# Two small tiles of norm gains trade places in SBUF with the softmax maxima, and the activation pair shifts by 64 bytes

## What is computed

```python
for l in range(DEPTH):                     # DEPTH = 2
    a = hybrid_mixer(rms_norm(x, pre_mix_g[l]), ...)      # latent attention + dilated windows
    x = x + rms_norm(a, post_mix_g[l])
    c = memory_cross_attention(rms_norm(x, pre_xattn_g[l]), rms_norm(mem, mem_g[l]), ...)
    x = x + rms_norm(c, post_xattn_g[l])
    hdn = jnp.square(jax.nn.relu(rms_norm(x, pre_mlp_g[l]) @ w_up[l]))     # 1024 -> 4096
    x = x + rms_norm(hdn @ w_down[l], post_mlp_g[l])                       # 4096 -> 1024
```

## Time and profile before

| | |
|---|---|
| median of three runs | 1260.73 us (1259.37 to 1261.54) |
| the profiled execution, its own time | 1259.12 us |
| its span, first to last instruction | 1257.3 us |
| PE busy / PEld busy | 1217.1 us (97%) / 1187.5 us (94%) |
| DVE / ACT / POOL busy | 830.6 us (66%) / 666.9 us (53%) / 47.9 us (4%) |
| DMA | 202.47 MB, mean 161 GB/s |
| granted TensorE clock, mean | 0.990 |

### The profile page before, as it was taken

How to read it: one execution, slowest core, us unless ns; L and a number is a source line. 1 busy time by engine, 2 the same in 40 slices (tenths; PEclk the granted TensorE clock), 3 DMA queues, 4 the chain that set the end, 5 groups by cost and what they waited for, 6 DMA issues and landing times.

```text
span 1257.3 us, 23250 instructions
## 1 busy us (share of the span) xinstructions
PE 1217.1 (97%) x10089; PEld 1187.5 (94%) x10089; DVE 830.6 (66%) x972; ACT 666.9 (53%) x969; POOL 47.9 (4%) x41
## 2 busy tenths in 40 slices
PE   7799999999999999999999999999999999999998
PEld 6799999999999999999899999999899997999998
DVE  5578548676664488863867766447778875676442
ACT  5376546455543356664555654444586754655331
POOL 2000000000000000000000000100200100000000
PEclk9899999999999999999999999999989998999999
DMA  7634545346656643455434765664551543466652
GB/s 229 207 107 141 185 146 165 95 143 201 211 188 206 189 123 118 135 168 167 136 101 139 218 212 171 220 216 134 150 165 46 166 137 101 135 202 201 201 184 85
DMA packets 197432, 202.47 MB, mean 161 GB/s; under 512 B 7703, under 2 KB 193842, under 8 KB 197331
## 3 DMA queue, kind: packets, MB, share of 16 engines
q1 hardware_dynamic: 193155, 195.50, 48.8%
q0 software_dynamic: 4176, 5.48, 1.5%
HBM read 199.88 MB, written 2.64 MB: 161 GB/s over the span
## 4 chain that ended last, share of the span: by engine, by line
PE 73%; DVE 10%; DMA 7%; ACT 7%; issue 3%; SPq 0%; DVEq 0%; ACTq 0%
PE bank L601 13%; PE bank L602 12%; PE bank L603 12%; PE bank L2569 5%; PE bank L2571 4%; PE bank L2567 4%; DVE w_lo L557 4%; DMA raw<-in_w_down_dram 3%; ACT w_hi L547 3%; PE bank L644 2%; PE bank L652 2%; PE bank L2477 2%; PE bank L646 2%; DMA raw<-in_w_in_dram 2%; PE bank L700 2%
## 5 line engine op out<-in xcount | busy, mean ns | idle before, releaser
L557 DVE TENSOR_TENSOR w_lo<-raw,w_hi 128x2048 fp32r<-128x2048 f32 (+6 forms) x208 | 419.8, 2028 | 264.2 <-ACT w_hi L547 263.9
L547 ACT ACTIVATE w_hi<-raw 128x2048 fp32r<-128x2048 f32 (+6 forms) x208 | 351.7, 1702 | 339.2 <-PE bank L2571 76.3
L601 PE MATMUL bank<-act_hi,w_hi 128*128 128x256 f32 (+1 forms) x1104 | 309.4, 280 | 10.3 <-DVE w_lo L557 10.3
L602 PE MATMUL bank<-act_lo,w_hi 128*128 128x256 f32 (+1 forms) x1104 | 307.4, 278 | 0.0
L603 PE MATMUL bank<-act_hi,w_lo 128*128 128x256 f32 (+1 forms) x1104 | 307.2, 278 | 0.0
L601 PEld LDWEIGHTS bank<-act_hi,w_hi 128*128 128x128 f32 (+1 forms) x1104 | 208.2, 189 | 12.7 <-issue 12.3
L602 PEld LDWEIGHTS bank<-act_lo,w_hi 128*128 128x128 f32 (+1 forms) x1104 | 208.5, 189 | 0.2
L603 PEld LDWEIGHTS bank<-act_hi,w_lo 128*128 128x128 f32 (+1 forms) x1104 | 208.5, 189 | 0.1
L2567 PE MATMUL bank<-h_hi,w_hi 128*128 128x256 f32 x736 | 203.6, 277 | 0.0
L2571 PE MATMUL bank<-h_hi,w_lo 128*128 128x256 f32 x736 | 203.5, 276 | 0.0
L2569 PE MATMUL bank<-h_lo,w_hi 128*128 128x256 f32 x736 | 203.5, 276 | 0.0
(11 more groups left out here) (418 smaller groups left out, 2166.0 us busy)
## 6 DMA issues: line engine op xcount, KB each, us to landing
raw<-in_w_up_dram SPq DMA_DIRECT2D x32, 1024.0 KB, 5.4
raw<-in_w_down_dram SPq DMA_DIRECT2D x32, 1024.0 KB, 5.4
raw<-in_w_ff_dram SPq DMA_DIRECT2D x32, 1024.0 KB, 5.4
raw<-in_w_in_dram SPq DMA_DIRECT2D x21, 1024.0 KB, 5.4
raw<-in_w_xk_dram SPq DMA_DIRECT2D x8, 1024.0 KB, 5.3
raw<-in_w_xv_dram SPq DMA_DIRECT2D x8, 1024.0 KB, 5.2
raw<-in_w_mix_out_dram SPq DMA_DIRECT2D x8, 1024.0 KB, 5.3
raw<-in_w_xq_dram SPq DMA_DIRECT2D x8, 1024.0 KB, 5.5
```

The costliest lines, as they stand in the source:

```text
L547: ins = act.activation(d, r, ACT.Copy)
L557: ins = dve.tensor_tensor(d, r, h.bitcast(F32), ALU.subtract)
L601: pe.matmul(o, stat_hi, mov_hi, start=first, stop=False)
L602: pe.matmul(o, stat_hi, mov_lo, start=False, stop=False)
```

## The change

Only the order of allocation changes. `g_pre` and `g_next` (96 + 32 = 128 bytes a partition) come to stand between `x_t` and `act_hi`, where `neg_max` (192 bytes) stood, and `neg_max` goes to their old place behind `g_all`.

```diff
         x_t = sb("x_t", [P, KD, T])
-        neg_max = sb("neg_max", [P, 48])
+        g_pre = sb("g_pre", [P, DEPTH + 1, 8])
+        g_next = sb("g_next", [P, 8])
         act_hi = sb("act_hi", [P, KD, T], F32R)
         act_lo = sb("act_lo", [P, KD, T], F32R)
         mem_t = sb("mem_t", [P, KD, T])
...
         g_all = sb("g_all", [P, DEPTH, G_PITCH])
-        g_pre = sb("g_pre", [P, DEPTH + 1, 8])
-        g_next = sb("g_next", [P, 8])
+        neg_max = sb("neg_max", [P, 48])
         g_cur = sb("g_cur", [P, G_PITCH])
```

## The result

The changed kernel takes 1278.82 us (median; 1277.74 to 1280.53, four runs) against 1261.06 us of the kernel before, run beside it: a ratio of 1.0138, with a 95% interval of 1.0121 to 1.0155. That is 17.8 us slower, outside the range of the prediction. It is close to the slower rival's figure, 1278.9 us, but it is reached in another way.

A forecast was written before the change was run, and what follows sets the result against it. TensorE bounds the kernel, busy 1217.1 of 1257.3 us, so matmul tempo matters. All terms were taken as 0, leaving the median of 1260.7 us as forecast, range 1254 to 1272 us.

The forecast's parts named there:

- the slower rival: Pair's new start loses the 113.3 ns tempo: up projections cost 8.9 us (1269.6), with down projections 18.2 us (1278.9); chance 0.32.
- PE's reads of the pair: Matmuls that move or hold `act`: effect of the new start between -10.6 and +18.2 us, taken as 0.
- the unknown: Matmul tempo: -10.6 us if every loose stretch turns tight, +18.2 us if up and down projections turn loose.
- the up runs' 8.9 us: The three up projections' 1926 matmuls turn from 113.3 to 117.9 ns each, 8.9 us more.
- The small tiles: ACT's reads of gains and maxima: 498 to 502 ns wherever they start, so their new places cost 0.
- ACT on the shifted pair: ACT's copies into `act_hi` at its new start: at most 0.5 us either way, taken as 0.
- The constants: Loads of `cst` and `toep` to addresses 64 bytes lower: gain at most 3.4 us, loss at most 1.9, taken as 0.
- the case in which the down runs follow them: Down projections inherit the up projections' loose tempo, 9.3 us more, 18.2 us together, 1278.9; 0.10 left out above the range.

The follow-up runs named there:

- the gains in front: Against the changed kernel: gains still before the pair, 64 bytes of gap put the pair back at 64, maxima last; 1261.64 us, ratio 1.0014.

## Why the prediction was wrong

**The step that failed** is the term for PE's reads of the pair: "I take 0, for this reason: the tempo isn't a function of the address alone." The premise was right and the inference wrong. At -64 the start of a stretch does choose between two tempos, as slabs 26 showed. But that both tempos are open at one distance says nothing of another, and at the distance of the change the tight one isn't on offer: of 112 stretches at distance 128 in all the traces none runs under 118.4 ns. The term, put at 0, measured 19.6 us of span in the traces. I had stated both ends of the unknown, -10.6 and +18.2 us, and then took the middle on evidence that came from one side only: every row I had of a moving activation was at -64, and the only rows at another distance, moving weights at +64, were all loose. Those 15 slabs against 0 tight ones were the best evidence in the trace that distance matters. The half slab at 187.3 us, which I set against them, was a stretch that inherited its tempo; it ended with the next stop. It did say truly that +64 allows both tempos, but +64 was not where the change would go.

**The rival's price** was right in sum and wrong in its parts. It had 8.9 us for the up projections and 9.3 us for the down projections. Measured: 10.2 us for the up projections, since the tempo there is 118.6 and not 117.9 ns, so 5.3 ns more and not 4.6; 1.7 us for the down projections, which found the tight tempo again by themselves in two MLPs of three; and 7.7 us in the attention stages. There the tight slabs of moving `act` turned too, some 1270 matmuls at 5.3 ns, and loose ones of moving `act` and moving weights, some 1750, went from 117.8 to 118.7 ns: 8.3 us by this count. What the attention stages lost was left out of the rival, and so was the slower third tempo; by luck they fill what the down projections lacked, and the sum that comes out right is no merit of the rival's. Its own distance doesn't fix whether a down projection turns: the third, at -64 throughout, is loose in the trace of the change, as in that of the pair alone at 0, and tight with the pair at 128. It also gave a wrong reason, an odd multiple of 64 as against an even one: the shift of everything by 192 bytes puts all pairs on an even multiple and costs nothing like it, and the pair at 192, an odd one, costs 1.2%.

**The rule on the gap.** The Trainium skill, "TensorE: Matmul & The Clock Gate", section "Back-to-back issue gap", has one gap for 256 columns, 109.2 ns, whatever the operands' starts, and gives it for an isolated matmul; for a stream with weight loads it has figures at 128 and 512 columns alone. The runs show 113.3 to 120.0 ns for the same instruction at full clock, by distance. I counted the rule as speaking against the slower rival; it should have had no weight once the trace showed two tempos.

**The terms that held.** The small tiles: 0 (the gains in front give 1.0014, with 1 inside the interval). ACT on the shifted pair: 501 ns for 502. Two readings under these terms were off, without effect: `g_pre` and `neg_max` both start at 128, so the rows show three places and not four, and 88 gained copies go into `act_hi`, not 96. The constants: they landed 2.0 us after issue, for 1.9, so the rule of the Trainium skill, "DMA: Bandwidth & Descriptors", section "How a descriptor splits into AXI transactions", on starts at multiples of 256 bytes shows nothing here, and PE's wait for them is 3.5 us for 3.4. PE's other waits shrank by about a microsecond.

**The range** ended at 1272, which by its own words "holds the up runs' 8.9 us and leaves out, with 0.10, the case in which the down runs follow them". The one-sided evidence should have moved the chance of 0.32 up, and the bound of +18.2 us, which I had worked out, should have been inside. Even that bound priced only the MLPs and only the two tempos seen so far.

## What to carry to other kernels

Where TensorE is the bound, as here, and fp32r operands of this shape move over held ones from SBUF, the order of allocation can be worth over 1%: measure it by counting matmuls in windows of equal length at full clock, pair by pair, and not by busy share, which stays at 97%. Take long windows or the starts themselves, since one count in 20 us is 0.7 ns. Any edit that adds or resizes a tile ahead of an operand moves the distance, so write it down and pad for it; here the moving tile wants to start 64 bytes below the held one, modulo 256, and 16 bytes off cost as much as 128. Whether other shapes and types want the same wasn't tried. When a trace shows two levels for one instruction and doesn't say why, an edit that touches the addresses should be forecast from the bounds, and not at zero.

## What the runs showed of the hardware that I had not expected

At a granted clock of 1.00 (2.4 GHz), matmuls of 256 fp32r columns with 128 held columns follow each other every 113.3 ns at best, and this only where moving minus held start is -64 or, seldom, +64 bytes modulo 256. By the starts in the timelines the moving pair has 120.0 ns at 0, 119.2 at -48, 119.3 at -80, 118.3 at -32 and 117.8 in the loose stretches at -64 and +64. Other distances have more than one tempo too: 118.7 or 120.0 at 128, 118.7 or 117.3 at -96, and 116.7 in three stretches at -48. Weights moving over the pair have 116.7 in most slabs at +32 and in all at +48, 118.1 at +80 and 120.0 at +96. What in the memory or in TensorE makes it so, the traces don't show.

At -64 two tempos are stable, 113.3 and 117.9 ns. A stretch takes one within its first half dozen matmuls and keeps it, over some 1390 of them at the longest, until PE pauses, if only for 50 ns, or until another pair of operands moves; in no trace does it change otherwise. In the trace of before, 21 of 38 stretches of moving activations that start without a lead-in are tight. With two, four or six matmuls of the weights on themselves directly ahead, all 65 stretches at this distance in the sixteen traces are. Such matmuls are themselves at a distance of 0, and the three down projections that follow directly on `act` at 0 (the pair at 128) are tight as well, as are the six that follow on `act` at -48 or -80, while of the six that follow on `act` at -32 or -96 five are loose. That what moved last sets the tempo of what comes next is a guess from this; why a lead-in chooses the tight one is open. Whether the toss falls otherwise in each execution, and so makes the scatter of this kernel's times, is open too: each trace is of one execution.
